# Order of work at three joints of a decoder layer: softmax transposes inside the next piece, the key-value up-projection with its own waits, the cross-attention residual turned later

## The reference

```
h = rmsnorm(x); q, ckv, k_rope, lru_x, lru_y, gate_mla, gate_lru = split(h @ w_in)
k_nope, v = split(rmsnorm(ckv) @ w_ukv)            # 16 heads, 128 + 128 columns, rank 512
q_rope, k_rope = rope(q_rope), rope(k_rope)        # cos and sin of the positions
p = softmax(mask((q . [k_nope, k_rope]) * scale)); o_mla = (p @ v) @ w_o_mla
o_lru = (rg_lru(conv(lru_x)) * gelu(lru_y)) @ w_o_lru
x = x + rmsnorm((sigmoid(gate_mla)*o_mla + sigmoid(gate_lru)*o_lru) @ w_out)
h = rmsnorm(x); mn = rmsnorm(mem)
cq, ck, cv = h @ w_cq, mn @ w_ck, mn @ w_cv        # 4 heads of 128
x = x + rmsnorm(softmax(cq . ck * scale) @ cv @ w_co)
x = x + rmsnorm(ffn(rmsnorm(x)))                   # w_up, causal conv, gelu gate, w_down
```

## Time and profile before

| | before |
|---|---|
| median of 3 runs | 1782.78 us (1782.33 to 1783.6) |
| the profiled execution, its own time | 1783.64 us |
| its span, first to last instruction | 1781.8 us |
| PE busy | 1754.2 us, 98% |
| PEld busy | 1494.5 us, 84% |
| DVE busy | 1142.1 us, 64% |
| ACT busy | 917.8 us, 52% |
| POOL busy | 148.7 us, 8% |
| mean granted TensorE clock | 0.997 |

### The profile page before, as it was taken

One profiled execution on the slowest core, in us unless ns is written; L12 is line 12 of the kernel. 1 busy time (PEld: TensorE's weight loads), 2 busy tenths in 40 slices (PEclk: granted clock), 3 DMA queues, 4 the chain that ended last, 5 costly groups with the idle time before them and its releaser, 6 DMA issues.

```text
span 1781.8 us, 25739 instructions
## 1 busy us (share of the span) xinstructions
PE 1754.2 (98%) x9129; PEld 1494.5 (84%) x9129; DVE 1142.1 (64%) x1403; ACT 917.8 (52%) x1186; POOL 148.7 (8%) x183
## 2 busy tenths in 40 slices
PE   8999999999999999999999999999999999999997
PEld 7888888888888888888888788888888888888886
DVE  6677775454788874445566567776467776467765
ACT  5566665343576763334447465555245555245552
POOL 0001110000244430000000001000000000000000
PEclk9999999999999999999999999999999999999999
DMA  7544457556455565555654335555555555555552
GB/s 237 196 131 142 141 166 255 200 199 195 153 171 182 184 228 189 191 200 190 221 190 164 119 118 189 188 188 201 197 168 188 188 188 202 196 168 188 188 207 100
DMA packets 214368, 325.80 MB, mean 183 GB/s; under 512 B 5888, under 2 KB 162212, under 8 KB 207268
## 3 DMA queue, kind: packets, MB, share of 16 engines
q1 hardware_dynamic: 208532, 315.53, 52.9%
q10 hardware_dynamic: 5776, 9.44, 1.5%
HBM read 322.85 MB, written 2.10 MB: 182 GB/s over the span
## 4 chain that ended last, share of the span: by engine, by line
PE 86%; issue 6%; DVE 4%; ACT 2%; POOL 1%; DMA 1%; SPq 0%; POOLq 0%; DVEq 0%; ACTq 0%
PE ps L482 40%; PE ps L530 39%; PE ps L498 2%; DVE wsp L1394 2%; PE ps L587 1%; PE ps L731 1%; ACT wsp L982 1%; POOL scr L1979 1%; PE ps L562 1%; PE ps L884 0%; PE ps L885 0%; DMA big_a<-in_x 0%; PE ps L694 0%; DMA raw<-in_w_in 0%; DVE big_a L1712 0%
## 5 line engine op out<-in xcount | busy, mean ns | idle before, releaser
L1394 DVE TENSOR_TENSOR wsp<-raw,wsp 128x2048 fp32r<-128x2048 f32 (+2 forms) x308 | 693.1, 2271 | 346.8 <-ACT wsp L982 343.8
L982 ACT ACTIVATE wsp<-raw 128x2048 fp32r<-128x2048 f32 (+2 forms) x308 | 574.1, 1886 | 309.3 <-PE ps L530 296.3
L482 PE MATMUL ps<-asp,wsp 128*128 128x512 f32 (+1 forms) x3072 | 545.0, 339 | 4.8 <-DVE wsp L1394 2.9
L482 PEld LDWEIGHTS ps<-asp,wsp 128*128 128x128 f32 x3072 | 470.9, 188 | 76.9 <-issue 3.6
L530 PE MATMUL ps<-wsp,hsp 128*128 128x512 f32 x2304 | 526.4, 390 | 0.2 <-DVE scr L1522 0.2
L530 PEld LDWEIGHTS ps<-wsp,hsp 128*128 128x128 f32 x2304 | 432.1, 188 | 89.6 <-issue 0.4
L482 PE MATMUL ps<-hsp,wsp 128*128 128x256 f32 (+1 forms) x1952 | 354.1, 341 | 2.7 <-DVE hsp L1448 1.9
L482 PEld LDWEIGHTS ps<-hsp,wsp 128*128 128x128 f32 x1952 | 300.0, 188 | 48.0 <-issue 2.5
L993 ACT ACTIVATE cr<-ps 128x256 f32<-128x256 f32 x189 | 70.1, 378 | 205.5 <-PE ps L482 173.8
L530 PE MATMUL ps<-wsp,asp 128*128 128x512 f32 x768 | 175.3, 389 | 0.0
L530 PEld LDWEIGHTS ps<-wsp,asp 128*128 128x128 f32 x768 | 144.0, 188 | 29.8
(11 more groups left out here) (194 smaller groups left out, 929.5 us busy)
## 6 DMA issues: line engine op xcount, KB each, us to landing
raw<-in_w_up SPq DMA_DIRECT2D x88, 1024.0 KB, 5.3
raw<-in_w_in SPq DMA_DIRECT2D x64, 1024.0 KB, 5.3
raw<-in_w_down SPq DMA_DIRECT2D x44, 1024.0 KB, 5.0
raw<-in_w_in SPq DMA_DIRECT2D x32, 768.0 KB, 4.4
raw<-in_w_o_mla SPq DMA_DIRECT2D x16, 1024.0 KB, 5.1
raw<-in_w_o_lru SPq DMA_DIRECT2D x16, 1024.0 KB, 5.1
raw<-in_w_out SPq DMA_DIRECT2D x16, 1024.0 KB, 5.0
raw<-in_w_ukv SPq DMA_DIRECT2D x8, 1024.0 KB, 5.3
```

What stands on the lines that cost most here:

```text
L482: mm = pe.matmul(ps[:, bank, 0:w], lhs(part, k), x[:, 0:w], start=(f and part == 0), stop=(l and n == 1))
L982: act.activation(wsp[:, p0 % SLOTS, 0, 0:n], raw[:, p0 % SLOTS, 0:n], ACT.Copy).then_inc(hi_done, 1)
L1394: dve.tensor_tensor(wsp[:, slot, 1, 0:n], raw[:, slot, 0:n], wsp[:, slot, 0, 0:n].bitcast(F32), ALU.subtract).then_inc(lo_done, 1)
```

## The change

The transposes of the probabilities are issued from inside piece 3: `q_piece` and `token_piece` take a function `halfway` and call it after the first of their tiles (after the first token half in the eighth round). The up-projection is written out, without a loop, on TensorE, ScalarE and VectorE; its first block has no claims and waits once for the raw rotary key's sum instead; ScalarE's conversion of its first piece stands ahead of the half turn, and the sines stand in the third block; VectorE makes the first block's key sums ahead of its subtraction, and the rotation of the key stands in the fifth block. The residual's tiles 8 to 15 are turned together after the last piece of the memory keys and evicted together ahead of the third conversion of the query phase.

```diff
-X2_TURNS = [range(0), range(8), range(8, 12), range(12, 16)]
-X2_EVICTS = [range(0), range(0), range(8), range(8, 12)]
+X2_TURNS = [range(0), range(8), range(0), range(8, 16)]
+X2_EVICTS = [range(0), range(0), range(8), range(0)]
...
-            def token_piece(ph, i, c, src, banks, back=4):
+            def token_piece(ph, i, c, src, banks, back=4, halfway=None):
...
                 for m in range(2):
+                    if halfway and m == 1:
+                        halfway()
...
-            def q_piece(ph, i, c):
+            def q_piece(ph, i, c, halfway=None):
...
                 for n, j in enumerate(Q_ORDER):
+                    if halfway and n == 1:
+                        halfway()
...
             def ukv(i):
                 for c in range(4):
+                    clear = i == 0 and c == 0
                     arrive(PH_UKV, i, c)
...
-                        claim(PH_UKV, i, 4 * c + j)
+                        if not clear:
+                            claim(PH_UKV, i, 4 * c + j)
...
-                        claim(PH_UKV, i, 4 * c + 2 + m)
+                        if not clear:
+                            claim(PH_UKV, i, 4 * c + 2 + m)
...
+            pe.wait_ge(tile_out, PH_A.t_end)
             pe.wait_ge(ckv_lo, RT)
-            rounds(pe, PH_UKV, ukv)
+            for i in range(PH_UKV.trips):
+                ukv(i)
...
-                for e in range(2):
-                    pe.wait_ge(probs_ready, u * 4 + 2 * e + 2)
-                    for b in range(3):
-                        mm = pe.transpose(ps[:, 5 + 2 * e, b * P:(b + 1) * P], PR[e][:, b * P:(b + 1) * P], ident[:, :])
-                    mm.then_inc(probs_turned, 1)
-                between(3)
+
+                def turn_probs():
+                    for e in range(2):
+                        pe.wait_ge(probs_ready, u * 4 + 2 * e + 2)
+                        for b in range(3):
+                            mm = pe.transpose(ps[:, 5 + 2 * e, b * P:(b + 1) * P], PR[e][:, b * P:(b + 1) * P], ident[:, :])
+                        mm.then_inc(probs_turned, 1)
+                between(3, turn_probs)
...
+            hi(PH_Q0, 0, 4)
             act.wait_ge(tile_out, 1)
             half_turn(KRAW)
-            act.wait_ge(angle_ready, 2)
-            act.activation(SIN, SIN, ACT.Sin).then_inc(table_ready, 1)
-            act.activation(COS, COS, ACT.Sin).then_inc(table_ready, 1)
-            hi(PH_Q0, 0, 4)
             hi(PH_Q0, 0, 5)
...
             def ukv(i):
                 for c in range(4):
+                    if (i, c) == (0, 2):
+                        act.wait_ge(angle_ready, 2)
+                        act.activation(SIN, SIN, ACT.Sin).then_inc(table_ready, 1)
+                        act.activation(COS, COS, ACT.Sin).then_inc(table_ready, 1)
                     hi(PH_UKV, i, c + LEAD)
...
             for c in range(4):
+                if c == 0:
+                    x2_high(range(8, 16))
                 hi(PH_CQ, 0, c + LEAD)
                 if c == 0:
-                    x2_high(range(12, 16))
                     x2_square(range(2))
...
-            dve.wait_ge(table_ready, 2)
-            rotate(1, KR, KRAW)

             def ukv(i):
                 for c in range(4):
-                    lo(PH_UKV, i, c + LEAD)
+                    if (i, c) != (0, 0):
+                        lo(PH_UKV, i, c + LEAD)
+                    if (i, c) == (1, 0):
+                        dve.wait_ge(table_ready, 2)
+                        rotate(1, KR, KRAW)
                     for j in range(2):
                         add(PH_UKV, i, 4 * c + j, bank=3 + j, dst=tile_at(big_a, i * 8 + 2 * c + j)).then_inc(tile_out, 1)
+                    if (i, c) == (0, 0):
+                        lo(PH_UKV, i, c + LEAD)
...
             for c in range(4):
+                if c == 0:
+                    x2_low(range(8, 16))
                 lo(PH_CQ, 0, c + LEAD)
-                if c == 0:
-                    x2_low(range(12, 16))
```

## The result

The changed kernel takes 1787.21 us in the median of 11 runs (1786.29 to 1788.67), the kernel before 1782.97 (1781.92 to 1783.6) in as many: ratio 1.0025, 95% interval 1.0016 to 1.0034. Forecast was 1786.5 in a range of 1783.6 to 1788.4. It is slower, by 4.2 us. The low end of the interval, 0.16%, lies under the 0.2% at which the prediction draws its line between slower and the same.

A forecast was written before the change was run, and what follows sets the result against it. TensorE, busy 98% of the span, bounds the kernel, so only its gaps count. Up-projection -0.7, attention +5.8 and memory keys -1.4 sum to +3.7 us on the median of 1782.78: 1786.5 us, range 1783.6 to 1788.4.

The forecast's parts named there:

- Up-projection: Key-value up-projection: three entry waits go, moved sines and rotation delay the fourth and sixth blocks; -0.7 us, bounds -1.7 and 0.
- The slack of 0.47: Up-projection blocks: 0.47 us from VectorE's first-tile sum at 91.92 to TensorE taking the freed bank at 92.44.
- Rival (c): Up-projection: sines and rotation fit into the slack because ScalarE idles over 1 us a block; +1.2 us, 1784.0; chance 0.09.
- (e): Up-projection's first block has to wait all the same, for something the claims hid; +3.7 + 2, 1788.5; chance 0.03.
- (d): Up-projection's third block: switching the table also drains ScalarE, 1.4 us more; +5.1 us, 1787.9; chance 0.05.
- Attention: Attention rounds: later transposes delay ScalarE's copies and so the next round's start, seven times; +5.8 us, bounds +4.5 and +6.5.
- TensorE's own gain: Attention rounds: the wait for GpSimd before the second three transposes goes, 2.6 us, but later copies swallow it.
- Rival (b): Attention rounds: the copies' delay does not reach the bank, so the kernel gets faster; -4.7 us, 1778.1; chance 0.07.
- Memory keys: Cross-attention keys: TensorE's wait for freed banks between third and fourth piece goes, nothing late behind; -1.4 us, bounds -1.5 and -0.7.
- The sum: Whole kernel: the three joints' terms add up to +3.7 us, giving 1786.5 us from the median; chance 0.76.

## Why the prediction was right

**Up-projection.** Right in each step: three entry waits gone, the first blocks at the beat, waits of 1.58 and 0.80 where 1.5 and 0.8 were forecast, in the fourth and sixth block. The slack of 0.47 behind the chain copy, conversion, subtraction, sum was the number that made it. The placing of the sines and the rotation in idle time confirms that the chain, and not the engines' load, was the price. Rival (c) is out by these waits, and (e) by the first block, which starts 8.57 us after the last 48 query matmuls (67.00 after 58.43), where 8.48 was reckoned without a wait. The time alone would not have told the forecast from (d): 1787.21 lies midway between 1786.5 and 1787.9. The trace puts (d) out too: in the changed kernel 0.64 us lie between the table load's end at 80.19 and the conversion at 80.83, with both sines in them, and the fourth block was late by the row's price. The drain of about 1.38 us that the Trainium skill gives for a switch of set ("ScalarE: Activation LUTs", "What ACT_TABLE_LOAD costs") doesn't show here either. Unrolling cost nothing to be seen: with the sines and the rotation placed, the fifth block starts 5.66 us after the fourth, across what was the turn of the loop.

**Attention.** Right in mechanism and size. The wait for GpSimd went in all rounds, TensorE's own gain was swallowed, and each round grew by the delay of ScalarE's copies. The kernel with the transposes alone gives the +5.7 by itself, and the one with the conversion first takes it away; no other edit was needed. The step on which the sum rests, that a copy comes 0.53 us after the first transpose when nothing else holds ScalarE, was read from one round; it held in all eight of the changed kernel (176.81 to 177.34 in the third). The single rounds came out less evenly than the sum, which owes something to errors that cancel: the first seven grew by 0.38, 1.03, 0.86, 0.87, 0.95, 0.87 and 0.88, where 0.42 and then 0.87 or 0.94 were forecast (0.15 of the 1.03 is the shorter time that the 48 query matmuls had in that round before). Rival (b) is out by the seven waits. What I passed over is that the kernel before already lost 0.3 a round to the same chain (0.35 by the kernel before with the conversion first), which is why mending it beats the kernel before. The row was in my hands, as 0.33 of idle, and I used it only as proof that there was no slack.

**Memory keys.** Right: 1.36 of 1.4, nothing given back.

**The sum.** 3.85 in the joints against 3.7. The medians differ by 4.24. The profiled executions themselves differ by 3.57 (1787.21 and 1783.64): 3.85 in the joints, 0.26 more ahead of them and about 0.5 less behind them. The rest is the spread of the runs. Part of that spread can be seen behind the query phase, where no edit reaches: there the granted clock is at half for a while in every trace, and longer in some executions than in others. Both profiled executions of this pair have the long one, the kernel with the transposes alone the short one (columns as above; 10 us each of the kernel before, the changed kernel and the kernel with the transposes alone):

```profile
1021.00:1031.00 10.00, 7.34 (x41) 7.34 (x42) 3.59 (x15) 2.33 (x8) 0.00 (x0) 0.66 0.00 0
1025.00:1035.00 10.00, 7.29 (x42) 7.30 (x43) 3.77 (x16) 2.33 (x8) 0.00 (x0) 0.66 0.00 0
1026.50:1036.50 10.00, 7.14 (x49) 7.14 (x50) 4.41 (x17) 3.10 (x11) 0.00 (x0) 0.83 0.01 2
```

By the end of these rows the last kernel has gained 1.2 us on the kernel before that no edit explains. The spread of the runs is as large as the distance to the bound of 0.2%, so the forecast of slower rather than same was right by less than the medians suggest.

## What to carry to other kernels

Before moving a step to where its own engine no longer waits, look at what stands behind the step's result on the next engine: with programs run in order, a copy that waits holds back every conversion behind it. Read from the chain whether that next engine has slack at this point (here 0), and move the unrelated work ahead of the waiting instruction in the same edit; then the move pays (2.8 us here), and without it it cost 5.8. Work that is hidden on average still costs its length less the slack if it stands in the chain that a block waits for (1.58 of the 1.92 us of the sines, 0.80 of the 1.25 of the rotation): put it behind the last instruction for which somebody waits.

## What the runs showed that was not expected

With a wait of 2.8 us in each of seven rounds, the granted clock went to half for a while in five of them, at 1.42 us each, on top of the wait; with waits of 1.4 it did not. And the 48 query matmuls at the start of a round took 8.43 us in some rounds and 8.58 in others of the same kernel, so a comparison of two rounds by their periods alone can be 0.15 off.
